# Transposing attention weights on TensorE instead of by DMA in a list-scheduled decoder layer on eight cores

## The reference

```python
zmix = rms_norm(h, mix_norm) @ w_mix_in          # gm_u | gm_v | q | k | v
gm_out = chunked_gmlp(gelu(gm_u), gelu(gm_v), ...)
# stick-breaking attention, 8 heads of 64, strictly causal, z = q.k / 8
log_1m = where(causal, -softplus(z), 0)
after = cumsum(log_1m, reverse=True) - log_1m
a = where(causal, exp(log_sigmoid(z) + after), 0)
sb_out = a @ v
h = h + concat([gm_out, sb_out]) @ w_mix_out
```

## Time and profile before

| | |
|---|---|
| median of 3 runs | 3923.32 us (3922.87 to 3926.26) |
| the profiled execution, its own time | 3923.32 us |
| its span, from the first to the last instruction | 3921.8 us |
| spans of the eight cores | 3907.8 to 3921.8 us |
| mean granted TensorE clock of the cores | 0.886 to 0.889 |
| PE, DVE, ACT, POOL busy | 83%, 62%, 36%, 30% of the span |
| DMA | 650.14 MB, 862605 packets, of which 636330 under 512 B; 576 transposing DMAs, 3.1 us to landing |

### The profile page before, as it was taken

How to read it: one execution, slowest core, us unless ns; L and a number is a source line. 1 busy time by engine, 2 the same in 40 slices (tenths; PEclk the granted TensorE clock), 3 DMA queues, 4 the chain that set the end, 5 groups by cost and what they waited for, 6 DMA issues and landing times.

```text
span 3921.8 us, 57434 instructions; the slowest of 8 cores (3907.8 to 3921.8 us)
## 1 busy us (share of the span) xinstructions
PE 3265.6 (83%) x14597; PEld 1377.1 (35%) x14597; DVE 2439.4 (62%) x2828; ACT 1399.8 (36%) x2625; POOL 1158.9 (30%) x1231
## 2 busy tenths in 40 slices
PE   6779787897979798897979889798897986986787
PEld 2234332343424343343424334243342432432233
DVE  3244454535574566656676577786777967978833
ACT  2242433322242333333343433434334433434422
POOL 1111112101221223232323334343343543545600
PEclk9989898897979899998979989799897997995598
DMA  8985599644565466764666556675576864865543
GB/s 273 319 270 153 161 312 291 172 136 113 153 174 151 113 153 154 182 166 111 165 153 171 143 124 174 161 181 143 132 169 162 187 140 109 183 140 104 94 141 95
DMA packets 862605, 650.14 MB, mean 166 GB/s; under 512 B 636330, under 2 KB 655314, under 8 KB 862290
## 3 DMA queue, kind: packets, MB, share of 16 engines
q1 hardware_dynamic: 860114, 644.36, 63.9%
q0 software_dynamic: 2176, 2.10, 0.4%
HBM read 436.03 MB, written 61.34 MB: 127 GB/s over the span
## 4 chain that ended last, share of the span: by engine, by line
PE 59%; DVE 16%; issue 8%; ACT 7%; SPq 4%; DMA 4%; POOL 1%; DVEq 1%; ACTq 0%; POOLq 0%
PE bank L175 59%; DVE P L208 8%; SPq L214 4%; ACT bank L188 2%; DVE xnT L205 2%; DMA AT<-A 1%; ACT L188 1%; DVE bank L197 1%; DMA fstv_96<-wts 1%; ACT rr L188 1%; DVE hT_56 L205 1%; DMA fstk_91<-wts 1%; ACT sq_65 L188 1%; DVE gvn L205 1%; DVE hT_55 L197 1%
## 5 line engine op out<-in xcount | busy, mean ns | idle before, releaser
L197 POOL TENSOR_TENSOR A<-P 128x1024 bf16<-128x1024 f32 (+3 forms) x576 | 1009.1, 1752 | 2282.8 <-DVE P L208 2025.7
L208 DVE TENSOR_TENSOR_SCAN P<-bank,P,cb 128x512 f32<-128x512 f32 x896 | 1148.7, 1282 | 433.0 <-ACT bank L188 343.1
L188 ACT ACTIVATE bank<-bank 128x512 f32<-128x512 f32 (+3 forms) x1152 | 583.2, 541 | 652.0 <-PE bank L175 650.3
L175 PE MATMUL bank<-AT,vc 128*128 128x256 bf16 x2112 | 377.7, 305 | 19.5 <-ACT sbT L188 11.9
L175 PE MATMUL bank<-kT,qT_54 64*128 64x512 bf16 (+3 forms) x640 | 197.0, 424 | 123.0 <-DVE P L208 120.9
L188 ACT ACTIVATE ef_63<-bank 128x512 f32<-128x512 f32 x240 | 142.9, 596 | 418.1 <-PE bank L175 399.0
L208 DVE TENSOR_TENSOR_SCAN P<-bank,cb 128x512 f32<-128x512 f32 (+3 forms) x256 | 210.5, 822 | 120.4 <-ACT bank L188 97.5
L175 PEld LDWEIGHTS bank<-AT,vc 128*128 128x128 bf16 x2112 | 200.6, 105 | 193.6 <-issue 102.1
L188 ACT ACTIVATE ef_64<-bank 128x512 f32<-128x512 f32 x240 | 142.7, 595 | 272.6 <-PE bank L175 241.9
L197 DVE TENSOR_TENSOR ef_63<-ef_63,bank 128x512 f32<-128x512 f32 x176 | 119.6, 679 | 153.0 <-ACT ef_63 L188 150.5
L197 DVE TENSOR_TENSOR ef_64<-ef_64,bank 128x512 f32<-128x512 f32 x176 | 119.3, 678 | 123.4 <-ACT ef_64 L188 116.5
(11 more groups left out here) (259 smaller groups left out, 4326.3 us busy)
## 6 DMA issues: line engine op xcount, KB each, us to landing
ring_74<-wscr SPq DMA_DIRECT2D x102, 256.0 KB, 3.0
ring_77<-wscr SPq DMA_DIRECT2D x101, 256.0 KB, 3.0
ring_68<-wscr SPq DMA_DIRECT2D x101, 256.0 KB, 3.0
ring_71<-wscr SPq DMA_DIRECT2D x101, 256.0 KB, 3.1
ring_72<-wscr SPq DMA_DIRECT2D x100, 256.0 KB, 3.0
ring_75<-wscr SPq DMA_DIRECT2D x100, 256.0 KB, 3.1
ring_78<-wscr SPq DMA_DIRECT2D x100, 256.0 KB, 3.0
ring_69<-wscr SPq DMA_DIRECT2D x99, 256.0 KB, 3.0
```

The source lines that it names most:

```text
L175: return lambda e: e.matmul(out, lhsT, rhs, start=start, stop=stop, skip_group_check=True)
L188: return lambda e: e.activation(out, in_, func, **kw)
L197: return lambda e: e.tensor_tensor(out, in0, in1, op)
L208: return lambda e: e.tensor_tensor_scan(out, d0, d1, initial, op0, op1)
```

## The change

Attention weights are no longer transposed by DMA. `stage_t` now issues, for each block of 128 keys that the item needs and each of its two heads, one PE transpose of a [128, 128] block of `A` (8 for a full item, 2 to 8 for a diagonal one) into bank 3, which becomes a bf16 bank of 1024 columns and is taken from the side stream's pool; then one ScalarE copy brings the bank to `AT` in SBUF. `AT` has two buffers and a contiguous [4, 256] layout. A round of the stream is now `stage_t(n - 2)`, `stage_a(n)`, `stage_v(n - 3)`. `sbT` and the gMLP output become the two halves of one buffer `mix` with two copies, and the gate `("O", ti - 1)` is gone, as is the zeroing of `A`. The side pool is 5, 6, 7; the wide pool has seven banks.

```diff
-SA = 2
-ST = 4
-LAG = 5
-    gmb = [salloc("gm%d" % i, [128, 4, T], BF16)[0] for i in range(2)]
-    sbT, _ = salloc("sbT", [128, 4, T], BF16)
+    mixb = [salloc("mix%d" % i, [128, 8, T], BF16)[0] for i in range(2)]
-    Ab, _ = salloc("A", [128, SA, 2, T], BF16)
-    ATb, _ = salloc("AT", [128, ST, 8, 128], BF16)
+    Ab, _ = salloc("A", [128, 2, 2, T], BF16)
+    ATb, _ = salloc("AT", [128, 2, 4, 256], BF16)
-        side = BankPool([3, 5, 6, 7])
-        wide = BankPool([0, 1, 2, 3, 4, 5, 6, 7])
+        side = BankPool([5, 6, 7])
+        wide = BankPool([0, 1, 2, 4, 5, 6, 7])
...
             for j in range(8):
                 w = rg.get(("mo", j))
                 b = bp.next()
-                for half, src in ((0, gmb[hb]), (1, sbT)):
-                    yield [w.res] + mres[4 * half:4 * half + 4] + ([bank_res[b]] if half == 0 else [])
...
+                for y in proj8(w, b, mixT, lambda k: [mres[k]]):
+                    yield y
...
-            done.add(("O", ti))
...
             def stage_t(n):
-                s = n % ST
-                sa = n % SA
-                S.op("sp", f_dmat(ATb[:, s, :, :], Ab[:, sa, :, :].rearrange("p h t -> p (h t)")), reads=[A_res[sa]], writes=[AT_res[s]], dma="t%d" % s, cost=1300.0)
+                s = n % 2
+                k0 = c_lo(n) // 128
+                for kb in range(k0, 4):
+                    for h in range(2):
+                        o0 = (kb * 2 + h) * 128
+                        S.op("pe", f_tr(banks[3][:, o0:o0 + 128], Ab[:, s, h, kb * 128:(kb + 1) * 128], identb), reads=[A_res[s], R_const], writes=[bank_res[3]], cost=76.0)
+                act(ATb[:, s, k0:4, :].rearrange("p a b -> p (a b)"), banks[3][:, k0 * 256:1024], AF.Copy, [bank_res[3]], [AT_res[s]])
...
-            for n in range(N + LAG):
+            for n in range(N + 3):
+                if 0 <= n - 2 < N:
+                    yield [A_res[n % 2], bank_res[3]]
+                    stage_t(n - 2)
                 if n < N:
...
                     stage_a(n)
-                m = n - LAG
-                if 0 <= m < N:
-                    ti = items[m][0]
-                    if items[m][3] == 0 and ti > 0 and items[m][1:3] == (0, 0):
-                        yield ("gate", ("O", ti - 1))
-                    yield [AT_res[m % ST], bank_res[4]]
-                    stage_v(m)
-                if 0 <= n - 1 < N:
-                    stage_t(n - 1)
+                if 0 <= n - 3 < N:
+                    yield [AT_res[(n - 3) % 2], bank_res[4]]
+                    stage_v(n - 3)
```

More of the change, by code:

```diff
@@ L214, in f_dma @@
     return lambda e: e.dma_start(out=out, in_=in_)
-def f_dmat(out, in_):
-    return lambda e: e.dma_start_transpose(out=out, in_=in_)
 def ffn_units(fi):
@@ L349, in build @@
     print("SBUF used %d of %d" % (off[0], top))
-    banks = [nc.alloc_psum_tensor("bank%d" % i, [128, 512], F32) for i in range(8)]
+    banks = [nc.alloc_psum_tensor("bank%d" % i, [128, 1024] if i == 3 else [128, 512], BF16 if i == 3 else F32) for i in range(8)]
     bank_res = [Res("bank%d" % i) for i in range(8)]
@@ L357, in build @@
     xnT_res = [Res("xnT%d" % k) for k in range(8)]
-    gm_resb = [[Res("gm%d_%d" % (i, k)) for k in range(4)] for i in range(2)]
-    sb_res = [Res("sb%d" % k) for k in range(4)]
+    mix_resb = [[Res("mix%d_%d" % (i, k)) for k in range(8)] for i in range(2)]
     q_resb = [[Res("q%d_%d" % (i, k)) for k in range(4)] for i in range(2)]
@@ L373, in build @@
     Pc_res = [Res("Pc%d" % i) for i in range(2)]
-    A_res = [Res("A%d" % i) for i in range(SA)]
-    AT_res = [Res("AT%d" % i) for i in range(ST)]
+    A_res = [Res("A%d" % i) for i in range(2)]
+    AT_res = [Res("AT%d" % i) for i in range(2)]
     scr_res = [Res("scr%d" % i) for i in range(NFF)]
@@ L385, in build @@
     scanm = cb[:, 256:896]
-    ALLRES = ([R_const, R_init, pT_res, rr_res, dum_res, ssq_res, rs1_res] + bank_res + sum(hT_resb, []) + xnT_res + sum(gm_resb, []) + sb_res
+    ALLRES = ([R_const, R_init, pT_res, rr_res, dum_res, ssq_res, rs1_res] + bank_res + sum(hT_resb, []) + xnT_res + sum(mix_resb, [])
               + sum(q_resb, []) + sum(kT_res, []) + v_res + ef_res + sq_res + ring_res + wscr_res + P_res + Pc_res + A_res + AT_res + scr_res)
@@ L436, in program @@
         S.op("sp", f_dma(cst[:, :], cst_d[:, :]), writes=[R_init], dma="c0")
-        S.op("pool", f_memset(Ab[:, :, :, :].rearrange("p a h t -> p (a h t)"), 0.0), writes=A_res)
         S.op("sp", f_dma(graw[:, :], norms_d[:, :]), writes=[R_init], dma="c1")
@@ L574, in mix_gen @@
             qT = qTb[hb]
-            mixT = gmb[hb]
-            mres = gm_resb[hb]
+            mixT = mixb[hb]
+            mres = mix_resb[hb]
             def q_evac(i, b):
@@ L651, in mix_out_gen @@
             hr = hres(hb)
+            mixT = mixb[hb]
+            mres = mix_resb[hb]
             nm = Norm(bp)
-            mres = gm_resb[hb] + sb_res
             for j in range(8):
@@ L656, in mix_out_gen @@
                 b = bp.next()
-                for half, src in ((0, gmb[hb]), (1, sbT)):
-                    yield [w.res] + mres[4 * half:4 * half + 4] + ([bank_res[b]] if half == 0 else [])
-                    for kk in range(4):
-                        k = 4 * half + kk
-                        mm(b, B(b), w.ap[:, k * 128:(k + 1) * 128], src[:, kk, :], k == 0, k == 7, [w.res, mres[k]])
+                for y in proj8(w, b, mixT, lambda k: [mres[k]]):
+                    yield y
                 if j > 0:
@@ L798, in stage_a @@
                     S.op("pool", f_copy(Pb[:, s, :, 0:1], Pb[:, 1 - s, :, T:T + 1]), reads=[P_res[1 - s]], writes=[Pc_res[s]], cost=150.0)
-                sa = n % SA
-                S.op("pool", f_tt(Ab[:, sa, :, c0:T], Pb[:, s, :, c0:T], Pb[:, s, :, c0 + 1:T + 1], ALU.subtract), reads=[P_res[s], Pc_res[s]], writes=[A_res[sa]], cost=2 * n_ * 1.65 + 205)
+                S.op("pool", f_tt(Ab[:, s, :, c0:T], Pb[:, s, :, c0:T], Pb[:, s, :, c0 + 1:T + 1], ALU.subtract), reads=[P_res[s], Pc_res[s]], writes=[A_res[s]], cost=2 * n_ * 1.65 + 205)
             def stage_t(n):
-                s = n % ST
-                sa = n % SA
-                S.op("sp", f_dmat(ATb[:, s, :, :], Ab[:, sa, :, :].rearrange("p h t -> p (h t)")), reads=[A_res[sa]], writes=[AT_res[s]], dma="t%d" % s, cost=1300.0)
+                s = n % 2
[5 more added lines that the diff above has]
+                act(ATb[:, s, k0:4, :].rearrange("p a b -> p (a b)"), banks[3][:, k0 * 256:1024], AF.Copy, [bank_res[3]], [AT_res[s]])
             def stage_v(n):
                 ti, hp, qb, kc = items[n]
-                s = n % ST
+                s = n % 2
                 k0 = c_lo(n) // 128
                 for kb in range(k0, 4):
-                    mm(4, B(4)[:, 0:256], vc[:, kc * 4 + kb, hp * 128:(hp + 1) * 128], ATb[:, s, kb::4, :], kc == ti and kb == k0, kc == 0 and kb == 3,
+                    mm(4, B(4)[:, 0:256], vc[:, kc * 4 + kb, hp * 128:(hp + 1) * 128], ATb[:, s, kb, :], kc == ti and kb == k0, kc == 0 and kb == 3,
                        [v_res[kc * 4 + kb], AT_res[s]])
@@ L816, in stage_v @@
                         r = slice(64 * h, 64 * h + 64)
-                        act(sbT[r, hp, qb * 128:(qb + 1) * 128], B(4)[r, h * 128:(h + 1) * 128], AF.Copy, [bank_res[4]], [sb_res[hp]])
+                        act(mixb[ti % 2][r, 4 + hp, qb * 128:(qb + 1) * 128], B(4)[r, h * 128:(h + 1) * 128], AF.Copy, [bank_res[4]], [mix_resb[ti % 2][4 + hp]])
                 if n + 1 == N or items[n + 1][0] != ti:
                     done.add(("A", ti))
-            for n in range(N + LAG):
+            for n in range(N + 3):
+                if 0 <= n - 2 < N:
+                    yield [A_res[n % 2], bank_res[3]]
+                    stage_t(n - 2)
                 if n < N:
```

## The result

The changed kernel takes 4194.52 us (median of 4 runs, 4193.42 to 4200.81), the kernel before 3923.48 us in the same comparison. The ratio is 1.0693, with a 95% interval of 1.0674 to 1.0711: 271 us slower. The forecast was 4148, within 4010 to 4290.

What follows compares the result with a forecast made beforehand. PE was taken to bound most of seven attention stages and the scan the end of the eighth. Six terms, 140 + 75 + 25 + 30 + 10 - 40 - 15 = +225 on 3923, gave 4148 us, range 4010 to 4290.

Steps and rivals of the forecast that it cites:

- Transposes on PE: Stages before the last tile's: 3246 transposes at 0.061 us take 198 us of PE, 30% hidden: +140 us.
- The last stage: Tail: a loop of transposes, copy, sigmoid and scans makes items 3.65 us instead of 2.79, with 8 more items: +75 us.
- One bank: Side stream with three banks instead of four: embedding gates lose 25 us, first FFN halves 30 us.
- ScalarE: Copies add 545 us to ScalarE, mostly covered by idle time; late squares and norms make PE wait: +10 us.
- The hand-over: From a tile's attention to its mixing output: last AV product 3 rounds later instead of 5, seven times: -40 us.
- The queues: SP and POOL queues lose the transposing DMAs and their waits; gain where weights first stream in: -15 us.
- banks do not decide: Rival: three banks stall each FFN gate and up pair by 0.5 us, giving 4272 us; chance 0.14.
- no gain of the hand-over shows: Rival: shorter hand-overs and transposes in idle PE make the kernel faster, 3866 us; chance 0.09.
- transposes overlap: Rival claimed the opposite: each transpose holds PE for a whole latency of 0.305 us, near 5000 us; chance 0.02.
- nothing evens out: Rival: the planner lets losses and gains cancel, 3905 to 3950 us; chance 0.05.

Runs made afterwards that it cites:

- e1: The changed kernel with one transpose per item in place of up to eight, the planner still counting all: span 4081.8 us, 1.0416 of the kernel before.
- e3: The changed kernel with rounds ordered scores n, AV n-3, transposes n-2, three buffers of `A`, one of `AT`: span 4063.7 us, 1.0334 of the kernel before.
- e4: The kernel before, DMA transposes kept, with bank 3 taken from the side and wide pools: span 3957.5 us, 1.0076 of the kernel before.
- e2: The changed kernel with ScalarE copies of 128 columns in place of 256 to 1024, planned as full: span 4115.9 us, 1.0464 of the kernel before.
- e5: The kernel before, DMA transposes kept, with the AV product 3 rounds after the scores in place of 5: span 3928.3 us, 1.0021 of the kernel before.

## Why the prediction was right, term by term

The sum was +225 and the result +271, with the right mechanisms in first place. But no term has its size: what the runs give for the six is about +95, +103, +36 to +43, +51, 0 and 0, and these overlap. That the total came so near is in part luck: 60 us too much in the first and the third term made up for part of what the others lacked.

*Transposes on PE, +140.* Right in kind, too high. The price of 0.061 us was near: 0.056 at full clock and 0.107 at the low one. By the Trainium skill's "TensorE: Matmul & The Clock Gate", section "Back-to-back issue gap", it would have been 0.081; the measurement decides against that here. Hidden was about half instead of 30%: e1 gains 84 of 157 us before the last stage, which for all 3246 transposes there makes some 95.

*The last stage, +75.* Right in mechanism, too small: 103. The step that was mis-sized is the loop's length. I had 7.3 us for two items and the trace shows 8.00. From the start of the eight transposes to the copy it is 1.17 us instead of 0.9, and three further hand-overs between engines add some 0.25 each: POOL 2.14 to the next transposes (1.90 of work), sigmoid 0.83 to the scan (0.58), scans 2.94 to POOL (2.67); I had put 0.2 for all of these. The 8 extra items for the tail were wrong: 59 and 58 items are left after the last embedding gate with attention beside it. The loop's pace shows instead in the mixed part: the items beside the first half of that stage's FFN come every 4.06 us, and that half takes 146 us where it took 117. e3 shows the loop by taking it away.

*One bank, +55.* Somewhat high (36 to 43 by e4), and the split is wrong. The embedding gates lose 41 instead of 25, the FFNs nothing instead of 30. The step that failed is the assumed 0.1 us per pair of FFN banks. That attention fills those waits, as I had said against the rival, would explain it; it was not shown.

*ScalarE, +10.* Too small. e2 finds 51 us of copying outside the last stage. I had counted idle time as cover and looked for the loss at the squares; 23 us of it are the next transposes' wait for the copy.

*The hand-over, -40.* The hand-overs shrank by 38 us in sum (155 to 117), and I find no gain from it: e5 shortens them by 47 and is no faster. In its stages 2 to 6 this holds with hardly a wait for transfers. A piece of work that is moved out of a stall is still to be done. This step of the prediction failed as far as e5 shows; it counted a shorter stall as a gain. In the changed kernel itself the lag was not varied.

*The queues, -15.* Nothing shows it: the first stage is 3 us shorter, while with DMA transposes alone it ranges from 461 (e5) to 478 us (e4). Whether DMA transposes cost anything while weights stream in was not tried by itself.

The single gains do not add up to 271. Without transposes 111, without copies 77, without the loop 129: 317 us, since the transposes and the copy are part of the loop. Taken together they are 262 (4193.1 to 3930.8). The rest, 9 us or 18 by the quickest executions, is the bank (36 to 43 us) less what the new round gives back; that last part was only seen as a remainder. The rivals: banks do not decide (e4), no gain of the hand-over shows (e5), transposes overlap (0.056 us), and nothing evens out.

## What to carry to other kernels

A transpose moved from a DMA to PE cost more here than its matmuls: the copy out of PSUM and the place of both in the in-order queues cost as much, so put the new pieces behind the work that the bounding engine waits for (e3: 129 of 271 us by another order and a third buffer of `A`). A stall that gets shorter because work leaves it need not be a gain: that work then runs elsewhere (e5, stages 2 to 6). And when a bank is freed, look first for the wait that uses it: here one line in the embedding gate was worth 1%.

## What the runs showed of the hardware that I had not expected

Changing between transposes and ordinary 128-row matmuls cost nothing: the first transpose after a 512-column matmul starts 0.216 us later and the first matmul after the last transpose 0.056, both medians in the trace of the changed kernel, the same as within either kind. The scores with their 64 rows do cost something: 0.152 us from a transpose to a score matmul, and 0.312 from a 512-column matmul in place of 0.216. And the granted clock did not fall with the transposes among the other matmuls: the stage of the earlier trace rows that had 0.90 now has 0.93.
